# A one-core encoder layer with a mixture of experts: matmul order in three places, the last load in quarters, and the last norm's rows broadcast by GpSimd

## The reference

```
h   = layer_norm(x)
mix = concat(windowed attention(h), bidirectional gated recurrence(h)) @ w_out
h1  = layer_norm(alpha * h + mix, ln1)
top 4 of 32 experts per token, softmax gates g
hid = h1 @ w_up[e] + b_up[e]          (1024 x 2048 per expert)
act = min(glu, 7) * sigmoid(1.702 glu) * (clip(lin) + 1)
ffn = sum over e of g[e] * (act @ w_down[e] + b_down[e])
out = layer_norm(alpha * h1 + ffn, ln2)
```

## Time and profile before

| | |
|---|---|
| median of 3 runs | 1073.86 us (1073.74 to 1074.52) |
| profiled execution, its own time | 1072.99 us |
| span of the profiled execution | 1071.2 us |
| granted TensorE clock, mean | 0.987 |
| busy: TensorE matmul / VectorE / ScalarE / GpSimd | 97% / 26% / 19% / 1% |
| read from HBM, rate over the span | 426.03 MB, 399 GB/s |
| chain that ended last | TensorE 73%, DMA 26%, VectorE 1% |

### The profile page before, as it was taken

One profiled execution on the slowest core, in us unless ns is written; L12 is line 12 of the kernel. 1 busy time (PEld: TensorE's weight loads), 2 busy tenths in 40 slices (PEclk: granted clock), 3 DMA queues, 4 the chain that ended last, 5 costly groups with the idle time before them and its releaser, 6 DMA issues.

```text
span 1071.2 us, 13106 instructions
## 1 busy us (share of the span) xinstructions
PE 1034.8 (97%) x5236; PEld 457.7 (43%) x5236; DVE 276.0 (26%) x717; ACT 207.1 (19%) x385; POOL 10.1 (1%) x27
## 2 busy tenths in 40 slices
PE   8999999999999999999999999999999999999997
PEld 8988784333333333333333333333333333334332
DVE  6888673111111111111111111011111111211043
ACT  5665421111111111111110111111111111011141
POOL 2000000000000000000000000000000000000000
PEclk9999999999999999999999999999999999999999
DMA  9583799999999999999999999999999999999996
GB/s 327 154 220 128 299 410 415 424 428 426 434 429 431 426 428 430 429 431 432 432 431 434 432 426 435 433 429 433 433 432 431 432 433 431 431 431 424 425 425 263
DMA packets 38624, 427.87 MB, mean 399 GB/s; under 512 B 4256, under 2 KB 17616, under 8 KB 20576
## 3 DMA queue, kind: packets, MB, share of 16 engines
q1 hardware_dynamic: 36864, 426.65, 95.2%
q10 hardware_dynamic: 1568, 0.44, 0.2%
q0 software_dynamic: 160, 0.32, 0.1%
HBM read 426.03 MB, written 1.57 MB: 399 GB/s over the span
## 4 chain that ended last, share of the span: by engine, by line
PE 73%; DMA 26%; DVE 1%; ACT 0%; issue 0%; POOLq 0%; ACTq 0%; DVEq 0%
PE bank L1866 29%; DMA pool_f<-in_w_down_dram 25%; PE bank L1932 16%; PE bank L1770 4%; PE bank L1489 4%; PE bank L1755 4%; PE bank L1506 3%; PE bank L1564 2%; PE bank L1763 2%; PE bank L1916 2%; PE bank L1880 1%; PE bank L1902 1%; PE bank L1534 1%; PE bank L1951 1%; PE bank L1470 0%; PE bank L1464 0%
## 5 line engine op out<-in xcount | busy, mean ns | idle before, releaser
L1866 PE MATMUL bank<-pool_f,bench 128*64 128x512 f32 x2048 | 453.6, 594 | 0.0
L1866 PEld LDWEIGHTS bank<-pool_f,bench 128*64 128x64 f32 x2048 | 144.1, 137 | 264.6 <-issue 255.7
L1932 PE MATMUL bank<-pool_f,bench 128*64 128x512 f32 x992 | 230.6, 619 | 23.3 <-DMA pool_f<-in_w_down_dram 23.3
L1932 PEld LDWEIGHTS bank<-pool_f,bench 128*64 128x64 f32 x992 | 75.6, 142 | 174.1 <-issue 152.5
L797 ACT ACTIVATE bench<-bench 128x256 f32<-128x256 f32 x64 | 26.6, 418 | 429.9 <-DVE bench L1342 429.9
L1342 DVE TENSOR_SCALAR bench<-bank 128x256 f32<-128x256 f32 x64 | 26.9, 420 | 296.5 <-PE bank L1866 296.5
L1324 DVE TENSOR_SCALAR bench<-iota_s,keyp,bench 128x128 f32<-128x128 f32 x62 | 18.6, 343 | 319.2 <-PE bank L1902 319.0
L1770 PE MATMUL bank<-bench,putT 64*128 64x512 f32 x248 | 61.6, 615 | 0.0
L1755 PE MATMUL bank<-X,bench 128*64 128x512 f32 x248 | 58.7, 592 | 0.0
L802 ACT COPY bench<-bank 128x512 f32<-128x512 f32 x31 | 18.2, 587 | 201.6 <-PE bank L1932 201.6
L1333 DVE TENSOR_SCALAR bench<-iota_s,keyp 128x64 f32<-128x64 f32 x60 | 12.5, 251 | 97.9 <-PE bank L1866 97.9
(11 more groups left out here) (323 smaller groups left out, 697.5 us busy)
## 6 DMA issues: line engine op xcount, KB each, us to landing
pool_f<-in_w_up_dram SPq DMA_DIRECT2D x41, 4096.0 KB, 30.3
pool_f<-in_w_down_dram SPq DMA_DIRECT2D x23, 4096.0 KB, 33.2
pool_f<-in_w_up_dram SPq DMA_DIRECT2D x40, 2048.0 KB, 19.8
pool_f<-in_w_down_dram SPq DMA_DIRECT2D x12, 2048.0 KB, 17.0
pool_f<-in_w_up_dram SPq DMA_DIRECT2D x12, 1024.0 KB, 9.9
pool_f<-in_w_down_dram SPq DMA_DIRECT2D x12, 1024.0 KB, 23.8
wbuf<-in_w_in_dram SPq DMA_DIRECT2D x9, 1024.0 KB, 8.5
bench<-in_w_in_dram SPq DMA_DIRECT2D x2, 1024.0 KB, 8.4
```

What stands on the lines that cost most here:

```text
L1866: ins = mm(bank[n][c * SLOTS:(c + 1) * SLOTS, :], xT[:, k, :], units(row, n, c), start=(k == 0), stop=(k == KT - 1))
L1932: ins = mm(bank[2][c * SLOTS:(c + 1) * SLOTS, :], actT[:, at:at + SLOTS], wk[:, a * D + c * 512:a * D + (c + 1) * 512], start=(i == 0 and ...
```

## The change

- **Mix order.** `mix_out` can take both column halves in one call (`BOTH`), with the order high x high for both, high x low for both, low weights last. The calls for tile 0, part 0 and tile 1, part 1 become such calls; in them `high_used` rises after the fourth of six products instead of the fifth, and `mix_done` of the first half after the fifth instead of the third. The other calls keep the order 0, 1, 2. VectorE does `normed(0, 0)` and `normed(0, 1)` ahead of `summed(1, 0)`.
- **ends_met** is called behind k = 3 of hidden(29), not k = 7.
- **Pass edge.** `put_back` and `gates_turned` leave `turn_over` and become `back`, which for the dynamic passes stands at the head of the next pass, behind the loop's edge. For the last one `gates_turned` is left out, and the scatter raises `put_ps` itself.
- **Last load.** The second down chunk of the last pass comes in a half and two quarters instead of two halves, with a wait (`last_in2`) ahead of the last quarter. `moments_paired(0)` moves behind a = 1 of the second chunk.
- **Last norm's rows.** SP loads both vectors as 4 KB each into partition 0 (`ln2row`, in the memory where the state comes later), directly behind the last fixed chunk, and GpSimd broadcasts them to all partitions. ScalarE waits for the broadcast ahead of the state copies.

```diff
+        ln2row = late[0:1, 0:2 * D]
...
-        STEPS += [("mix", 0, (0, 0)), ("mix", 0, (0, 1)), ("o", 0, 0), ("o", 1, 0), ("catT", 2, 0), ("mix", 0, (1, 0)), ("catT", 3, 0)]
-        STEPS += [("mix", 0, (1, 1)), ("mix", 1, (1, 0)), ("mix", 1, (1, 1))]
+        STEPS += [("mix", 0, (0, BOTH)), ("o", 0, 0), ("o", 1, 0), ("catT", 2, 0), ("mix", 0, (1, 0)), ("catT", 3, 0)]
+        STEPS += [("mix", 0, (1, 1)), ("mix", 1, (1, BOTH))]
...
-            sp.wait_ge(s["chunk_used"], used(down_at(FIXED - 2, DNC - 1)))
+            sp.wait_ge(s["chunk_used"], used(SMALLER - 1))
             for i, v in enumerate((ln2_g, ln2_b)):
-                sp.dma_start(ln2p[:, i, :], v[0].partition_broadcast(P)).then_inc(s["ln2_in"], 16)
+                sp.dma_start(ln2row[:, i * D:(i + 1) * D], v[0:1, :]).then_inc(s["ln2row_in"], 16)
...
-            for c in range(DNC):
-                load_down(sp, LAST_HOME[c], e, c, s[f"last_in{c}"])
+            load_down(sp, LAST_HOME[0], e, 0, s["last_in0"])
+            for i, there in enumerate((chunk_in[LAST_HOME[1]], s["last_in1"], s["last_in2"])):
+                w = slice((0, 2, 3)[i] * D, (2, 3, 4)[i] * D)
+                sp.dma_start(buffer(LAST_HOME[1])[:, w], source(e, UPC + 1)[:, w]).then_inc(there, 16)
...
+            pool.wait_ge(s["ln2row_in"], 32)
+            g.partition_broadcast(lncat[:, 0:2 * D], ln2row).then_inc(s["ln2_in"], 1)
...
+            act.wait_ge(s["ln2_in"], 1)
             for t in range(TT):
                 for n in range(2):
                     a.copy(state_sb[:, t, n * 512:n * 512 + 512], bank[4 + 2 * t + n][:, :]).then_inc(s["state_out"], 1)
...
             inverted(0)
-            summed(1, 0)
             normed(0, 0)
             normed(0, 1)
+            summed(1, 0)
...
-                first, middle, final = (0, 2, 1) if t == part_ else (0, 1, 2)
-                for i in (first, middle, final):
+                if n == BOTH:
+                    order = ((0, 0), (2, 0), (0, 1), (2, 1), (1, 0), (1, 1))
+                else:
+                    order = ((0, n), (1, n), (2, n))
+                for i, m in order:
...
+                        if i == 1 and a == 3:
+                            pe.wait_ge(s["last_in2"], 16)
...
+                        if i == 1 and a == 1:
+                            moments_paired(0)
                     ins.then_inc(s["chunk_used"], 1)
-                    if i == 0:
-                        moments_paired(0)
-
-            MET_AT = KT - 1
+
+            MET_AT = 3
...
-                put_back(p, turn)
-                gates_turned(p)
+
+            def back(p, final=False):
+
+                put_back(p, final)
+                if not final:
+                    gates_turned(p)
...
             with pe.Fori(FIXED, last_pass) as p:
+                back(p - 1)
                 hidden(p)
                 turn_over(p)
+            back(last_pass - 1, final=True)
```

More of the change, by code:

```diff
@@ L267, in encoder_layer @@
         first_pick = putT[:, 0:TT * SLOTS].rearrange("p (t n) -> p t n", t=TT)
-        names = ("x_in0 x_in1 emb_in rows_in ln1_in ln2_in par_in "
+        names = ("x_in0 x_in1 emb_in rows_in ln1_in ln2_in ln2row_in par_in "
                  "att_out_in rec_out_in bias_in braw_in bias_left bup_split zeroed consts h_ready lb_ps proj_done job_done logf_ready logf_in exps_in "
@@ L277, in encoder_layer @@
                  "out_high_ready out_low_ready att_high_ready att_low_ready rec_high_ready rec_low_ready "
-                 "half_in0 half_in1 last_in0 last_in1 plan_read put_ready xT_ready actT_ready y_ready glu_ready lin_ready sig_ready act_ready "
+                 "half_in0 half_in1 last_in0 last_in1 last_in2 plan_read put_ready xT_ready actT_ready y_ready glu_ready lin_ready sig_ready act_ready "
                  "state_out ends_ready ends_ps ends_in where_ready rows_out gains_in base_done slot_moments pair_ps pair_var pair_std rows_ready state_normed stored dve_step act_step pool_step tail_step half_used").split()
@@ L299, in encoder_layer @@
         BATCH = [(t, g) for t in range(TT) for g in range(NG)]
+        BOTH = 2
         def two(kind, b):
@@ L849, in _ @@
             preload(ACT.Sqrt)
-            act.wait_ge(s["ln2_in"], 32)
+            act.wait_ge(s["ln2_in"], 1)
             for c in range(2):
@@ L1392, in state_normed @@
             def state_normed():
-                dve.wait_ge(s["ln2_in"], 32)
+                dve.wait_ge(s["ln2_in"], 1)
                 for t in range(TT):
@@ L1539, in mix_out @@
             def mix_out(t, part_, n):
-                if part_ == 0 and n == 0:
+                if part_ == 0 and n in (0, BOTH):
                     pe.wait_ge(proj_read[GI["zg" if t == 0 else "ih"]], 1)
@@ L1562, in mix_out @@
                         pe.wait_ge(s["att_low_ready"], 2 - t)
+                    final = order[-2 + m][0] if n == BOTH else 2
                     for k in range(4):
-                        ins = mm(bank[4 + 2 * t + n][:, :], cp[:, k, :], wp[:, k * D + n * 512:k * D + (n + 1) * 512],
-                                 start=(part_ == 0 and i == first and k == 0), stop=(part_ == 1 and i == final and k == 3))
-                    if i == 2 and t == part_ and n == 1:
+                        ins = mm(bank[4 + 2 * t + m][:, :], cp[:, k, :], wp[:, k * D + m * 512:k * D + (m + 1) * 512],
+                                 start=(part_ == 0 and i == 0 and k == 0), stop=(part_ == 1 and i == final and k == 3))
+                    if n == BOTH and (i, m) == (2, 1):
                         ins.then_inc(s["high_used"], 1)
-                if part_ == 1:
-                    ins.then_inc(s["mix_done"], 1)
-                elif n == 1:
+                    if part_ == 1 and i == final:
+                        ins.then_inc(s["mix_done"], 1)
+                if part_ == 0 and n in (1, BOTH):
                     ins.then_inc(s["mix_half"], 1)
@@ L1764, in gather_turned, with scatter @@
                 ins.then_inc(s["xT_ps"], 1)
-            def scatter(start=False, stop=False, rows_of=ysb):
+            def scatter(start=False, final=False, rows_of=ysb):
                 for q in range(4):
                     r = slice((q % 2) * SLOTS, (q % 2 + 1) * SLOTS)
-                    mm(bank[4 + q][:, :], putT[r, (q // 2) * P:(q // 2 + 1) * P], rows_of[r, :], start=start, stop=stop)
+                    ins = mm(bank[4 + q][:, :], putT[r, (q // 2) * P:(q // 2 + 1) * P], rows_of[r, :], start=start, stop=final)
+                if final:
+                    ins.then_inc(s["put_ps"], 1)
             def ends_met():
@@ L1883, in hidden, with put_back @@
                         between[k]()
-            def put_back(p, turn=None):
+            def put_back(p, final=False):
                 if isinstance(p, int) and p == 0:
@@ L1893, in put_back @@
                 else:
-                    scatter(stop=not isinstance(p, int) and turn is None)
+                    scatter(final=final)
                 if isinstance(p, int) and p == RESIDUAL:
```

1 line of the change is left out of this document (added).

## The result

| | before | after |
|---|---|---|
| median | 1074.24 us (1073.74 to 1075.32, 6 runs) | 1085.43 us (1082.75 to 1089.8, 6 runs) |
| profiled execution, its own time | 1072.99 us | 1082.75 us |
| span of the profiled execution | 1071.2 us | 1081.0 us |

The ratio is 1.0109, with a 95% interval from 1.0095 to 1.0122: 11.2 us slower, where 2.8 us faster was forecast. The profiled execution of after is the fastest of its six; its span is 9.8 us longer.

The account below looks back on a forecast made before the run. Until 989.23 us the weight stream was taken as the limit, then TensorE alone. 0.9 + 1.58 + 0.37 - 0.07 = 2.8 us, subtracted from the median 1073.86, gave 1071.1 us, range 1070.4 to 1073.4.

Parts of the forecast that it names:

- the last norm's rows: Behind the last stall: 2.4 us less weight stream, no time by itself, only cover for the last loads; broadcast hidden.
- 14.5 us of room: Broadcast time taken as hidden, between the two rows landing at about 1017.6 us and ScalarE's state copies.
- the elementwise row: Nearest trace row for the broadcast's length: 0.62 us for 512 columns, 2.5 us for 2048.
- Rival 4: A long broadcast stops TensorE ahead of the state's gather; at 22 us +4.7 us, 1078.6 us; chance 0.14.
- The pass edge: Scatter and transposes behind the loop's edge: registers and increments covered under the gather, costing nothing, 0.3 us if uncovered.
- The 0.37 us of the transposes left out: gates_turned not issued for the last pass, on TensorE's path: 0.37 us gained.
- The stream's start: Mix phase: high_used rises earlier, two weight loads are issued 0.91 us earlier, the whole stream comes 0.9 us earlier.
- ends_met: At k = 3 of hidden(29): clock stays up, pass 28's down product takes 6.87 instead of 8.45 us; 1.58 us gained.
- Rival 1: The clock falls inside hidden(29), after ends_met at its new place; 2.0 us gained, 1071.9 us; chance 0.23.
- no wait for the last loads: After 989 us TensorE waits for no load; slack left 0.8 us for the first, 1.9 us for the last.
- The last load's quarters: Last down chunk of the last pass: saves up to 0.9 us where the last load binds; it doesn't, so nothing.
- moments_paired: At the end, moments_paired(0) moves 1.7 us later and VectorE's first rows end later: +0.07 us.

Follow-up runs that it names:

- only_broadcast: The kernel before with only the last norm's rows loaded to one partition and broadcast by GpSimd; 1085.15 us beside 1073.66 of before, ratio 1.0107.
- edge_alone: The kernel before with only the scatter and transposes moved behind the loop's edge, the last transposes left out; 1077.98 us beside 1073.48, ratio 1.0038.
- runs 4 and 12: library_back_early_regs (1073.5 us, ratio 0.9997) and edge_early_regs (1073.41 us, ratio 0.9994).
- all_but_broadcast: The kernel after with the last norm's rows loaded by DMA to all partitions as before; 1074.97 us, ratio 1.0000 to before.
- library_back: The kernel after with one more instruction, loading GpSimd's standard library again behind the broadcast; 1075.34 us, ratio 1.0014 to before.
- library_back_early_regs: library_back with TensorE's eight semaphore increments and register load behind the down product of pass 28, ahead of its gather; 1073.5 us, ratio 0.9997 to before.
- ends_at_3_alone: The kernel before with only ends_met moved behind k = 3 of hidden(29); 1073.53 us beside 1073.48, ratio 0.9998.
- mix_order_alone: The kernel before with only the new mix order and the order of VectorE's norm steps; 1074.33 us beside 1073.48, ratio 0.9998.
- edge_early_regs: edge_alone with the eight increments and the register load behind the down product of pass 28; 1073.41 us beside 1073.93 of before, ratio 0.9994.

## Why the prediction was wrong

**The step that failed: the last norm's rows.** The prediction says that this part "gives no time by itself", and prices the broadcast only by its own duration, against up to 14.5 us of room. All of that held: 2.31 us, hidden, near the 2.5 us of the elementwise row as chosen. But the instruction also changes what stands in GpSimd when the program ends, and this comes back at the start of the next execution, as 11.3 to 11.6 us ahead of the identity matrix, a place where nothing hides it: the term for the start of the program was nothing, and it measured 10.3 us on the path of after and 11.5 us in the median of only_broadcast (the masked instruction of the earlier trace rows is of the same operation, and its 0.6 us tell nothing of that). Rival 4 had the sign and the part of the diff right and the mechanism and place wrong; its chance of 0.14 is no credit to it. The Trainium skill (GPSIMD Engine Reference, Instruction dispatch) had a part of what was missing: a first call to freshly loaded code pays about 6 us. I set it beside the broadcast and asked how much room was there. The question that I left out is what other code has to be loaded because of it. By that figure, an estimate, the start would have lost about 6 us; the traces show 11.26 to 11.58, and the measured number decides.

**The pass edge, mis-sized.** The 0.37 us of the transposes left out were gained as forecast. But "nothing, 0.3 us if that cover is gone" was 1.65 us, plus a fall of the clock in some executions: 4.5 us in the median alone (edge_alone), 1.8 us on top of the other edits. The prediction had the sequencer run some dozen instructions ahead "under the gather". It can be that far ahead, but not there: it reaches the block at the last transposes, which wait for ScalarE, and only their 0.75 us cover its 2.4 us. In runs 4 and 12 the block stands ahead of that wait, its register load runs at 995.8 and 995.1 us under the down product, and there is no idle time ahead of the scatter. Why the same edit costs 4.5 us alone and is not to be seen in the sum of all but the broadcast (ratio 1.0000, interval up to 1.0031) isn't settled; that comparison has the widest interval of all, with runs from 1071.91 us at a mean clock of 0.989 to 1079.5 at 0.984.

**The stream's start, right in place, unseen at the end.** Both loads came 0.9 us earlier, and the stream kept that until about 385 us. At 989 us 0.2 us of it are left on average, with executions of either order up to 1.6 us and more apart. The ratio is 0.9998, give or take 1.3 us: a gain of 0.9 us is neither shown nor excluded.

**ends_met.** Rival 1 (the clock falls inside hidden(29)) came in three of five profiles with the new place and the thin matmuls in one piece: all_but_broadcast, library_back and library_back_early_regs, but not in after and ends_at_3_alone. Where it stayed up, the step was right: 6.88 and 6.87 instead of 8.45 us. In five pieces it stayed up over hidden(29) in all three profiles. Still the median of ends_at_3_alone is that of before; its profiled execution, with the clock up, is the fastest of its twelve.

The prediction tied the fall at 989 us to thin work and wait together. The profiles with `ends_met` at its old place say that the wait isn't needed: of six, only before waited for the load (0.82 us); the others waited 0.43 us for ScalarE's copy of the results, and the down product still took 8.56 to 8.78 us in three of these five (mix_order_alone, only_broadcast, edge_early_regs) and 7.09 in two. So thin matmuls in one piece were followed by the lower clock in seven of eleven profiles, at either place, and in five pieces in none of three. That makes the undivided piece the likely cause; so few profiles don't prove it. The rule that the prediction took from the earlier trace rows, that the clock falls behind long stalls and not behind short ones, holds mostly: even in before it stayed up behind one of 2.22 us, at 784.12.

**The rest** held: no wait for the last loads behind 999 us in after; the copies didn't wait for the broadcast. The last load's quarters and `moments_paired` weren't tried by themselves.

**Was it all of one profile?** The sum took 1.58 us off for a fall that before's one profiled execution had. Executions of before took 1071.3 to 1076.3 us in the last set of runs, and the pattern of stalls and clock varies; a term that stands on one fall of the clock should have had the chance that an execution has it. The same goes for the last stall at 989 us, from which the prediction counted: thirteen of fourteen profiles don't have it.

## What to carry to other kernels

An instruction from another GpSimd code library can cost more than its duration: look at what GpSimd does first in the program, since that is where the old code must come back, and load the standard library again behind the special one, where GpSimd is idle. Register loads and semaphore increments of the engine that sets the end belong where a long piece of its work is already issued, not behind a wait of the sequencer with only a short piece to cover them. And a gain of one clock fall, or of 1 us in the start of a stream that runs for 850 us, is below what executions differ by.

## What the runs showed of the hardware

- GpSimd's code outlives the execution: 11.26 and 11.58 us ahead of the first masked instruction when the program ends on the broadcast's library (only_broadcast, after), 0.24 us in the eight profiles without the broadcast, 0.49 us in the four in which the standard library is loaded back. The seven `MEMSET`s of GpSimd before it weren't held up.
- `PARTITION_BROADCAST` of 2048 float32 from one partition to 128 takes 2.30 to 2.31 us in all six profiles that have it.
- TensorE's sequencer issues semaphore increments 0.15 us apart and spends 0.48 us on a register load from SBUF (before and after). This costs TensorE nothing as long as matmuls issued earlier still run.
- Behind 90 of 112 stalls of over 2 us the next product took 1.7 us longer, which makes some 3.4 us at the lower clock (an estimate); it did so behind none of 88 under 1 us (fourteen profiles).
- Thin matmuls for 2.4 us in one piece, with full ones on both sides, are at times followed by the lower clock, with no stall near. After library_back's, over 982 to 986 us:

```profile
982.00:986.00 4.00, 4.00 (x16) 1.58 (x17) 0.00 (x0) 0.34 (x3) 0.00 (x0) 0.60 0.95 410
```
